# First stage of a two-block transformer kernel: x loaded by halves of columns and turned with both row blocks in one bank, four weight units in pieces, tables on ScalarE

## What is computed

```python
# layer 0 of the first block
hn  = rmsnorm(h, norm_mix[0])                 # h = x
qkv = hn @ w_qkv                              # w_qkv is 1024 x 3072
q, k, v = split(qkv, 3)
lam  = exp(sum(lq1*lk1)) - exp(sum(lq2*lk2)) + lam_init
bias = -slopes[:, None, None] * abs(qpos - kpos)     # slope of head h is 2**-(h+1)
s = q @ k.T * scale + bias;  a = softmax(s);  a = a[0] - lam * a[1]

# second block, on the 16 meta tokens, known from the start
rms_norm(meta_tokens, norm_mix_g)
```

## Time and profile before

| | before |
|---|---|
| median of 3 executions | 1027.63 us (1026.58 to 1028.51) |
| profiled execution, its own time | 1026.79 us |
| span of the profiled execution | 1025.0 us |
| mean granted TensorE clock | 0.994 |
| TensorE busy | 1000.1 us (98%) |
| VectorE busy | 642.6 us (63%) |
| ScalarE busy | 502.8 us (49%) |

### The profile page before, as it was taken

How to read it: one execution, slowest core, us unless ns; L and a number is a source line. 1 busy time by engine, 2 the same in 40 slices (tenths; PEclk the granted TensorE clock), 3 DMA queues, 4 the chain that set the end, 5 groups by cost and what they waited for, 6 DMA issues and landing times.

```text
span 1025.0 us, 13901 instructions
## 1 busy us (share of the span) xinstructions
PE 1000.1 (98%) x5549; PEld 854.9 (83%) x5549; DVE 642.6 (63%) x980; ACT 502.8 (49%) x742; POOL 125.6 (12%) x207
## 2 busy tenths in 40 slices
PE   7999899999999999999999999999999999999996
PEld 7889678888888898988888888888889888888885
DVE  6867577655556775555765555578665877545553
ACT  6566564444344655544544444455664354344432
POOL 5000598700000000000000000012500000000000
PEclk9999999999999999999999999999999999999999
DMA  9944359865555554343475555545633238555611
GB/s 271 299 135 141 98 117 234 274 200 182 188 194 176 185 186 149 119 124 123 145 244 172 199 183 187 194 133 178 204 145 124 86 124 282 165 190 180 199 47 41
DMA packets 112864, 174.72 MB, mean 170 GB/s; under 512 B 5992, under 2 KB 73584, under 8 KB 112800
## 3 DMA queue, kind: packets, MB, share of 16 engines
q1 hardware_dynamic: 106512, 165.69, 50.3%
q0 software_dynamic: 6272, 8.15, 3.2%
q10 hardware_dynamic: 16, 0.00, 0.0%
HBM read 172.77 MB, written 1.05 MB: 170 GB/s over the span
## 4 chain that ended last, share of the span: by engine, by line
PE 86%; DVE 8%; ACT 3%; issue 1%; DMA 1%; SPq 0%; ACTq 0%; DVEq 0%
PE bank L948 26%; PE bank L950 25%; PE bank L949 25%; DVE wl L1414 3%; PE bank L1061 2%; PE bank L1139 2%; PE bank L1091 1%; PE bank L1116 1%; PE bank L963 1%; DMA raw<-in_da_w_qkv_dram 1%; PE bank L1122 1%; ACT wh L597 1%; PE bank L1109 1%; PE bank L1071 1%; PE bank L1094 0%
## 5 line engine op out<-in xcount | busy, mean ns | idle before, releaser
L1414 DVE TENSOR_TENSOR wl<-raw,wh 128x2048 fp32r<-128x2048 f32 x154 | 355.5, 2315 | 178.1 <-ACT wh L597 177.9
L597 ACT ACTIVATE wh<-raw 128x2048 fp32r<-128x2048 f32 x154 | 292.1, 1910 | 111.6 <-PE bank L950 107.5
L948 PE MATMUL bank<-wh,xh 128*128 128x512 f32 (+1 forms) x792 | 300.9, 380 | 5.6 <-DVE xl L1478 3.2
L950 PE MATMUL bank<-wh,xl 128*128 128x512 f32 (+1 forms) x792 | 295.7, 373 | 0.0
L949 PE MATMUL bank<-wl,xh 128*128 128x512 f32 (+1 forms) x792 | 295.7, 373 | 0.0
L948 PEld LDWEIGHTS bank<-wh,xh 128*128 128x128 f32 x792 | 148.9, 188 | 31.8 <-issue 6.1
L950 PEld LDWEIGHTS bank<-wh,xl 128*128 128x128 f32 x792 | 148.8, 188 | 27.4
L949 PEld LDWEIGHTS bank<-wl,xh 128*128 128x128 f32 x792 | 149.0, 188 | 25.3
L948 PE MATMUL bank<-wh,ah 128*128 128x512 f32 x320 | 127.4, 398 | 0.0
L950 PE MATMUL bank<-wh,al 128*128 128x512 f32 x320 | 125.1, 391 | 0.0
L949 PE MATMUL bank<-wl,ah 128*128 128x512 f32 x320 | 124.8, 390 | 0.0
(11 more groups left out here) (233 smaller groups left out, 873.0 us busy)
## 6 DMA issues: line engine op xcount, KB each, us to landing
raw<-in_w_ff_dram SPq DMA_DIRECT2D x32, 1024.0 KB, 5.2
raw<-in_ffn_w_gate_dram SPq DMA_DIRECT2D x44, 512.0 KB, 4.1
raw<-in_ffn_w_up_dram SPq DMA_DIRECT2D x44, 512.0 KB, 5.0
raw<-in_ffn_w_down_dram SPq DMA_DIRECT2D x22, 1024.0 KB, 5.0
raw<-in_na_w_qkv_dram SPq DMA_DIRECT2D x12, 1024.0 KB, 5.2
raw<-in_w_in_dram SPq DMA_DIRECT2D x12, 1024.0 KB, 5.2
raw<-in_da_w_qkv_dram SPq DMA_DIRECT2D x11, 1024.0 KB, 11.5
raw<-in_ple_w_gate_dram SPq DMA_DIRECT2D x8, 1024.0 KB, 5.1
```

Source lines behind the costliest of these rows:

```text
L597: nc.scalar.activation(wh[:, i % RING, :], raw[:, i % RAW, :], ACT.Copy).then_inc(s_hi, 1)
L948: nc.tensor.matmul(dst, lh, rh, start=start, stop=False, skip_group_check=True)
L950: return nc.tensor.matmul(dst, ll, rh, start=False, stop=stop, skip_group_check=True)
L1414: nc.vector.tensor_tensor(wl[:, i % RING, :], raw[:, i % RAW, :], wh[:, i % RING, :].bitcast(F32), ALU.subtract).then_inc(s_lo, 1)
```

## The change

x is loaded in two halves of 512 columns, each as two loads of 128 rows, and the second half is issued between the second and the third piece of unit 0. The two row blocks of a column block are turned side by side in one bank, so that the gain is applied to 128x256 in one instruction. The second half of x is turned inside `first_pair`, after its second block. Units 0 to 3 (`PIECED`) are loaded in four pieces each and split in four blocks each. On TensorE `spread_root` moves behind quarter k0. On ScalarE the squares come between the blocks of unit 2, and the 8 tables are made there. On VectorE the distances and lambda come later, the meta tokens come behind `q_over_rms(0)`, and unit 4 and unit 5 are split behind `k_out(0)`.

```diff
+PIECED = 4
@@ sync
-            for b in range(TB):
-                sp.dma_start(h[:, b, :], t["x"][0].rearrange("(b p) n -> p b n", p=P)[:, b, :]).then_inc(s_x[b], 16)
+            def load_x(c):
+                cols = slice(512 * c, 512 * c + 512)
+                for b in range(TB):
+                    sp.dma_start(h[:, b, cols], t["x"][0].rearrange("(b p) n -> p b n", p=P)[:, b, cols]).then_inc(s_x[c], 16)
+
+            load_x(0)
...
-                if i == 0:
+                if i < PIECED:
+                    n = dst.shape[1] // 4
                     for k in range(4):
-                        sp.dma_start(dst[:, k, :], units[0][0][2][:, k, :]).then_inc(s_first[k], 16)
+                        sp.dma_start(dst[:, n * k:n * k + n, :], units[i][0][2][:, n * k:n * k + n, :]).then_inc(s_piece[i][k], 16)
+                        if (i, k) == (0, 1):
+                            load_x(1)
@@ scalar
+            for k in range(4):
+                gained_hi(0, k)
+            for k in range(4):
+                split_block(0, k)
             for k in range(4):
+                gained_hi(1, k)
                 split_block(1, k)
-            split[0] = 2
-            split_to(3)
-            for b in range(TB):
-                for c in range(2):
-                    square("mix0", b, c, hn[:, b, 512 * c:512 * c + 512])
+            for k in range(4):
+                split_block(2, k)
+                square("mix0", k // 2, k % 2, hn[:, k // 2, 512 * (k % 2):512 * (k % 2) + 512])
+            for k in range(4):
+                split_block(3, k)
+            split[0] = PIECED
...
+            spread_root("mix0", bank[4])
+            split_to(5)
             act.wait_ge(s_lamr, 1)
             nc.scalar.activation(lam[:, 2:4], lam[:, 0:2], ACT.Exp).then_inc(s_lamr, 1)
+            act.wait_ge(s_abs, 1)
+            for hd in range(8):
+                ins = nc.scalar.activation(near[:, hd, :], dist_f, ACT.Copy, scale=-(2.0 ** -(hd + 1)))
+            ins.then_inc(s_slopes, 1)
@@ tensor
+            def first_turns(c):
+                pe.wait_ge(s_x[c], 32)
+                for k in range(4):
+                    for b in range(TB):
+                        ins = nc.tensor.transpose(first_bank(c, k)[:, b * P:(b + 1) * P],
+                                                  h[:, b, (4 * c + k) * P:(4 * c + k + 1) * P], ident[:, :])
+                    ins.then_inc(first_turned.sem, 1)
...
+                        if (kh, k) == (0, 1):
+                            first_turns(1)
...
-                spread_root(mix, bank[4])
-                run(quarter("k", 0))
+                if l == 0:
+                    run(quarter("k", 0))
+                    spread_root(mix, bank[4])
+                else:
+                    spread_root(mix, bank[4])
+                    run(quarter("k", 0))
 
                 if l == 0:
                     meta_turn()
@@ vector
+            for c in range(2):
+                for k in range(4):
+                    gained_lo(c, k)
+                    split_block(c, k)
+            for k in range(4):
+                split_block(2, k)
+            diagonal("mix0", row_roots("mix0", EPS))
             for k in range(4):
+                split_block(3, k)
+            split[0] = PIECED
...
                 u = first["q", l, 0]
-                split_to(u + 2 + 3)
-                q_over_rms(0)
-                split_to(first["k", l, 0] + 4)
-                k_out(0)
+                if l == 0:
+                    distances()
+                    lambda_sums()
+                    q_over_rms(0)
+                    meta_norm()
+                    wait(dve, normed, "meta", 0, 0)
+                    k_out(0)
+                    split_to(u + 2 + 3)
...
-                if l == 1:
+                if l == 0:
+                    split_to(first["k", l, 0] + 4)
+                    dve.wait_ge(s_lamr, 2)
+                    nc.vector.tensor_scalar(lam[:, 0:1], lam[:, 2:3], lam[:, 3:4], LAM_INIT, ALU.subtract,
+                                            ALU.add).then_inc(s_lamr, 1)
+                    dve.wait_ge(s_lamr, 3)
+                    dve.wait_ge(s_slopes, 1)
```

More of the change, by code:

```diff
@@ L235, in two_blocks_kernel @@
         for l in range(3):
-            TURNS += [(f"mix{l}", *k) for k in CB] + ([("meta", 0, 0)] if l == 0 else [])
+            TURNS += [(f"mix{l}", *k) for k in CB] if l else [("meta", 0, 0)]
             TURNS += [(f"att{l}", b, c) for c in range(2) for b in range(2)]
@@ L317, in two_blocks_kernel @@
         s_pe = sem("pe_own")
-        s_x = [sem(f"x_landed{b}") for b in range(TB)]
+        s_x = [sem(f"x_columns_landed{c}") for c in range(2)]
         s_gain = [sem(f"gain_landed{i}") for i in range(2)]
-        s_first = [sem(f"first_unit_landed{k}") for k in range(4)]
+        s_piece = [[sem(f"unit{u}_piece{k}_landed") for k in range(4)] for u in range(PIECED)]
         s_gain_first = sem("gain_first_landed")
@@ L624, in turns_hi, with gained_hi @@
                     turn_hi(name, b, c)
[L626 to L635, removed]
+            def gained_hi(c, k):
+                wait(act, first_turned, c, k)
+                nc.scalar.activation(xh[:, 4 * c + k, X0:XP], first_bank(c, k), ACT.Copy,
+                                     scale=gain_cols[:, 4 * c + k:4 * c + k + 1]).then_inc(first_hi.sem, 1)
             def split_block(u, k):
+                act.wait_ge(s_piece[u][k], 16)
                 nc.scalar.activation(wh[:, u, 512 * k:512 * k + 512], raw[:, u, 512 * k:512 * k + 512],
@@ L789, in _ @@
                 split_to(u + 2 + 3)
-                spread_root(f"mix{l}", bank[4])
+                if l == 1:
+                    spread_root("mix1", bank[4])
                 q_out(0)
@@ L958, in turn @@
             def turn(name, b, c):
-                if c == 1 and name != "mix0" and not name.startswith("att"):
+                if c == 1 and not name.startswith("att"):
                     need(name, b, 0)
@@ L1023, in first_pair @@
                     for k in range(4):
[L1024 to L1028, removed]
+                        wait(pe, first_lo, kh, k)
                         pe.wait_ge(s_lo, 4 * kh + k + 1)
@@ L1675, in _ @@
-            for b in range(TB):
-                first_turn_lo(b, 1)
-            for k in range(4):
-                split_block(1, k)
-            split[0] = 2
-            split_to(3)
-            diagonal("mix0", row_roots("mix0", EPS))
-            wait(dve, sumsq, "meta", 0, 0)
-            dve.wait_ge(s_meta, 32)
-            link(nc.vector.tensor_scalar(stat[0:META, 40:41], stat[0:META, 40:41], EPS_2, None, ALU.add))
-            inv_root(rstd[0:META, 20:21], stat[0:META, 40:41])
-            nc.vector.scalar_tensor_tensor(out=meta_n, in0=meta_s, scalar=rstd[0:META, 20:21], in1=meta_gain,
-                                           op0=ALU.mult, op1=ALU.mult).then_inc(normed.sem, 1)
@@ L1708, in _, with distances, lambda_sums @@
-            dve.wait_ge(s_lamr, 3)
+                split_block(3, k)
+            split[0] = PIECED
+            def distances():
+                dve.wait_ge(s_dist, 1)
+                link(nc.vector.tensor_copy(dist_f, dist_i))
+                link(nc.vector.tensor_scalar(dist_n, dist_f, -1.0, None, ALU.mult))
+                nc.vector.tensor_tensor(dist_f, dist_f, dist_n, ALU.max).then_inc(s_abs, 1)
+            def lambda_sums():
+                dve.wait_ge(s_lamv, 64)
+                for m in range(2):
+                    ins = nc.vector.tensor_tensor_reduce(out=lam_out, in0=lams[:, 2 * m, :], in1=lams[:, 2 * m + 1, :],
+                                                         scale=1.0, scalar=0.0, op0=ALU.mult, op1=ALU.add,
+                                                         accum_out=lam[:, m:m + 1])
+                    if m == 0:
+                        link(ins)
+                ins.then_inc(s_lamr, 1)
@@ new lines, in meta_norm @@
+            def meta_norm():
+                wait(dve, sumsq, "meta", 0, 0)
+                dve.wait_ge(s_meta, 32)
+                link(nc.vector.tensor_scalar(stat[0:META, 40:41], stat[0:META, 40:41], EPS_2, None, ALU.add))
+                inv_root(rstd[0:META, 20:21], stat[0:META, 40:41])
+                nc.vector.scalar_tensor_tensor(out=meta_n, in0=meta_s, scalar=rstd[0:META, 20:21], in1=meta_gain,
+                                               op0=ALU.mult, op1=ALU.mult).then_inc(normed.sem, 1)
```

104 lines of the change are left out of this document (30 added, 74 removed).

## The result

| | before | after |
|---|---|---|
| median | 1027.63 us (1025.28 to 1029.32, 7 runs) | 1030.5 us (1029.33 to 1031.36, 7 runs) |
| span of the profiled execution | 1025.0 us | 1028.9 us |
| mean granted TensorE clock | 0.994 | 0.993 |

The account below looks back on a forecast made before the run. TensorE bounds the kernel, busy 1000.1 of 1025.0 us. Scores of step 0 come 4.3 later, k1 saves 1.5, net +2.8 on 1027.63: 1030.4 us, range 1028.6 to 1032.2.

Parts of the forecast that it names:

- Front: x by halves, turned in pairs: products start at 8.3, 0.9 earlier, but q ends at 22.7 against 22.48; bounds 22.2 to 23.2.
- Rival B: Clock favours the new front, rising by 9.5 instead of 12.95, worth 1.5 us: +1.3, 1028.9; chance 0.14.
- wait (c): Before k0, `spread_root` waits for the diagonal, TensorE 0.34 idle, about 0.4 us; forecast gone with `spread_root` behind k0.
- The new wait: TensorE idle 29.3 to 34.15 ahead of `meta_turn`, 4.85 us, for meta tokens normed behind `q_over_rms(0)`; `meta_turn` 4.8 later.
- The clock behind it: Behind the idle 4.85 us the clock falls; v0 starts at 35.6, low to 39.2, ends at 42.95: +1.85 us.
- k_out, tables, pieces: k ready at 34.9, ahead of the scores at 43.0; eight tables, 4 us on ScalarE, cost nothing; late loads hidden.
- Stall (d): TensorE idle 2.37 us ahead of step 0's scores, released by `k_out`, plus 1.5 of low clock in k1: 3.9, removed.
- Rival C: No wait at `meta_turn`; stalls (c) and (d) and both clock losses gone: -4.2, 1023.4; chance 0.05.
- Rival D: Clock low longer behind the 4.85 us, or ScalarE's tables delay VectorE past the scores: +4.0 to +5.5, 1032.2; chance 0.19.

Follow-up runs that it names:

- busy front: Eight matmuls nobody reads added around the first turns of x: changed kernel 1028.49 us (ratio 1.0015), kernel with three moves 1022.83 us (0.9956).
- single exchange: Kernel before with `k_out(0)` ahead of the split of unit 5 on VectorE in layer 0: 1026.29 us, ratio 0.9986.
- both: Kernel before with `k_out(0)` ahead of the split of unit 5 and attention step 0 ahead of unit 6 on VectorE: 1023.94 us, ratio 0.9967.
- the front experiment: Changed kernel with eight matmuls nobody reads, four ahead of the first turns of x and four behind them: 1028.49 us, ratio 1.0015.
- the first experiment: Changed kernel with the norm of the meta tokens moved ahead of the distances on VectorE: 1029.79 us, ratio 1.0017.
- the reordered kernel: Changed kernel: meta norm ahead of distances, step 0 ahead of units 5 and 6 (VectorE), embedding and turned meta tokens ahead of unit 5 (ScalarE): 1024.42 us, 0.9974.
- the last wait: Changed kernel with the three moves and eight additional front matmuls, `meta_turn` also moved behind v0: 1022.27 us, ratio 0.9948.

## Why the prediction was right, point by point

**The time** was forecast as 1030.4 and measured as 1030.5. That it agrees to 0.1 us is luck: the interval alone is 1.6 to 4.0 us, and two misses cancel in part.

**Front.** First product 8.3, measured 8.62. The end of q was to stay near 22.5 and was forecast at 22.7; it came at 23.7 (`spread_root` 29.49, less 48 products of k0). The step that missed is the rise of the clock, left at 12.95 and measured at about 14.5, among the second turns of x, whose spacing falls from 0.21 to 0.11 us there. By the last instruction at the lower spacing, it rose at 12.99, 10.19 and 9.82 in three profiles with the old front, between 11.1 and 14.6 in seven with the new one, and between the last additional matmul and the first products with the busy front. The new front leaves TensorE idle for 1.9 us or more ahead of the first product (0.5 to 0.7 before). So the first row of the change's gain, 0.6 us earlier products, was worth less than nothing in this profile. Rival B pointed at the right knob and the wrong way.

**spread_root and wait (c).** Right: no wait there. But its price was read from one profile, the one in which the clock rose latest. In the other two with the old front (single exchange, then both) q ended 1.3 to 1.4 us earlier, and `spread_root` waited for the diagonal until the same time:

```profile
22.83 0.70 PE L1043 MATMUL bank<-pt,ones 128*128 128x256 f32 x2 [1.51 <-DVE pt L1469]
22.93 0.70 PE L1043 MATMUL bank<-pt,ones 128*128 128x256 f32 x2 [1.71 <-DVE pt L1469]
```

So in the old order the diagonal took up what an early clock gave, and `meta_turn` started at 29.2 to 29.35 in all three. In the new order nothing does: `spread_root` started anywhere from 27.9 to 29.6 in seven profiles, and the next step can follow 0.44 behind it (28.94 to 29.38 with `meta_turn` behind v0). The middle of the seven is level with the old order, and the changed kernel's profile is among the late ones.

**The new wait.** Forecast 4.85 us idle, measured 4.73, released by the instruction that was named. The chain took 5.3 us (29.49 to 34.81) against 5.55. That it follows `spread_root` was shown by the front experiment, and that it is the place of the norm on VectorE by the first experiment (0.91 left).

**The clock behind it.** v0 started at 36.38 and ran low to 38.4, 2 us instead of 3.6; the low clock cost 1.5 instead of 1.85. This made up for some of the late front: scores at 43.22 against 43.0.

**k_out, tables, pieces.** Stall (d) went and k1 ran at full speed (46.92 - 43.22 = 3.70 for its first half, as forecast). Loading units 1 to 3 in pieces costs and brings nothing, shown in the reordered kernel only. Ahead of unit 4 the kernel before makes 9 issues, not 7 (two for x, four for unit 0, three more); nothing in the sum hangs on it. The tables cost nothing in the change as made, only argued from VectorE's wait of 0.43 at step 0.

**What the prediction did not see.** Rival C priced the change without the wait at -4.2 us, and stall (d) at 3.9. Both left out the next thing in line. In the sum the removal of stall (d) was booked as -2.37 - 1.5, and it held only because the new wait was longer: with the wait gone the same kernel reached 1029.8 or 1028.5, above the kernel before in the first case and not to be told from it in the second (0.9998 to 1.0017), for `row_neg` of step 0 behind units 5 and 6. I asked of `k_out`'s queue what stands ahead of it, and not of the next consumer's. The new wait therefore is one of two bounds. With it in place the second does not show: no bracket stands at the scores of step 1, and VectorE even waits 0.43 us for those of step 0. With it gone the second takes most of the gain back. Only both together brought the kernel below the one before; the second alone was not taken out of the changed kernel, so that it would bring nothing there is read from the trace and not run.

**Rival D** did not come; the tables (3.40 us on ScalarE for eight) did delay the embedding on VectorE, by 0.33 us here and 1.88 in the first experiment.

## What to carry to other kernels

When a step is moved behind an operation that waits for a product of TensorE, look whether TensorE has an in-order wait for the moved step: here this turned 3 us of hidden work and 1.3 us beside it into 4.7 us of idle time. Price a removed stall only up to the next consumer in the same queue: the exchange of two steps on VectorE moved the scores of step 2 by 1.7 us, and a second exchange, of the step behind it, by another 1.3. Do not count an earlier start as gained before the clock has been looked at: here the first product came 0.6 us earlier and the last product of q 1.25 us later (23.61 against 22.36).

## What was not expected of the hardware

Eight matmuls that nobody reads, about 4 us of work around the first turns of x, brought 1.6 us in the reordered kernel. In the changed kernel, with TensorE busy from 2.4 us on but for 0.19 us ahead of the first product, the products ran at 120 ns from 8.6, where with idle stretches of 2.3 and 1.9 us they had been 213 ns apart until 13.9. The additional matmuls and the turns among them were still 213 ns apart; the rise came between the last of them (7.8 to 8.1) and the second product (8.6 to 9.0) in all three profiles. The turns of x alone (4.42 to 8.50 in the kernel before) had not lifted the clock ahead of the first product in any of the ten profiles without additional matmuls in the front. Whether it is the closed gaps or the kind of work, matmuls beside transposes, these runs do not separate.

Where the clock rises moved from profile to profile by 3.2 us with the old front (9.8 to 13.0) and by 3.5 with the new one (11.1 to 14.6). At 0.44 us lost for each us at the lower level the latter is 1.5 us, more than the pieces or the last wait are worth, and a reason to compare medians of many executions rather than spans. A rise that moves like this fits what the Trainium skill ("TensorE: Matmul & The Clock Gate", Part 1) says of a monitor that is not reset by the start of a kernel; no run here shows the monitor itself.
